# Two-block network on one core: modulation chunks loaded behind the first attention, expert weights in the state stage

## The reference, cut to what matters

```python
c_act = silu(c)
sh1, sc1, gt1, sh2, sc2, gt2 = split(c_act @ w_mod + b_mod, 6)
h = layer_norm(x) * (1 + sc1) + sh1
y = hybrid_mixer(h)       # chunked state-space scan (SSD) and forgetting attention, gated and merged, @ w_o
x = layer_norm(alpha * x + (1 + gt1) * y, ln1_g, ln1_b)
h = layer_norm(x) * (1 + sc2) + sh2
y = hierarchical_moe(h)   # 16 experts, 2 picked per token: (silu(h @ w_gate) * (h @ w_up)) @ w_down
x = layer_norm(alpha * x + (1 + gt2) * y, ln2_g, ln2_b)
```

## Time and profile before

| what | value |
|---|---|
| time, median of 3 runs | 1687.82 us |
| the three runs | 1689.45, 1684.5, 1687.82 us |
| span of the profiled execution, first to last instruction | 1684.1 us |
| its mean granted TensorE clock | 0.992 |
| PE busy | 1594.6 us |
| DVE busy | 936.2 us |
| ACT busy | 655.0 us |
| bytes read from HBM | 330.94 MB |

### The profile page before, as it was taken

One profiled execution on the slowest core, in us unless ns is written; L12 is line 12 of the kernel. 1 busy time (PEld: TensorE's weight loads), 2 busy tenths in 40 slices (PEclk: granted clock), 3 DMA queues, 4 the chain that ended last, 5 costly groups with the idle time before them and its releaser, 6 DMA issues.

```text
span 1684.1 us, 22446 instructions
## 1 busy us (share of the span) xinstructions
PE 1594.6 (95%) x9391; PEld 1239.9 (74%) x9391; DVE 936.2 (56%) x1380; ACT 655.0 (39%) x962; POOL 27.4 (2%) x89
## 2 busy tenths in 40 slices
PE   5999999989999879999999999999999999999998
PEld 1998655454445468687888899988768778889986
DVE  3876666632222266466675566545456567556653
ACT  2543420111111144565644534435355644544441
POOL 1000010100000000000000000000000000000000
PEclk9999999999999989999999999999999999999999
DMA  9555518999999924423354356545424235536651
GB/s 310 193 177 200 202 55 296 332 383 404 393 357 410 389 97 150 125 70 131 127 197 154 122 179 200 193 152 199 144 85 150 101 125 176 174 120 194 200 176 74
DMA packets 165376, 333.29 MB, mean 198 GB/s; under 512 B 17699, under 2 KB 69157, under 8 KB 165285
## 3 DMA queue, kind: packets, MB, share of 16 engines
q1 hardware_dynamic: 159728, 326.94, 54.2%
q10 hardware_dynamic: 5558, 5.06, 0.9%
HBM read 330.94 MB, written 1.05 MB: 197 GB/s over the span
## 4 chain that ended last, share of the span: by engine, by line
PE 77%; DVE 10%; DMA 7%; ACT 4%; issue 1%; POOL 0%; ACTq 0%; SPq 0%; POOLq 0%; DVEq 0%
PE ps_g L726 19%; PE ps_g L707 15%; PE ps_g L1262 5%; PE ps_g L1130 5%; DMA arena<-in_w_up_dram 4%; PE ps_s L1518 4%; PE ps_p L1518 3%; PE ps_o L774 3%; PE ps_g L867 3%; DVE ring_r L2266 2%; PE ps_p L707 2%; DMA ring<-in_w_mod_dram 1%; PE ps_x L680 1%; PE ps_g L1485 1%; PE ps_g L1406 1%
## 5 line engine op out<-in xcount | busy, mean ns | idle before, releaser
L2266 DVE TENSOR_TENSOR ring_r<-ring,late_w 128x4096 fp32r<-128x4096 f32 (+1 forms) x50 | 217.0, 4339 | 153.4 <-ACT late_w L1834 153.4
L1834 ACT ACTIVATE late_w<-ring 128x4096 fp32r<-128x4096 f32 (+1 forms) x50 | 178.1, 3563 | 126.8 <-PE ps_p L1518 42.8
L726 PE MATMUL ps_g<-hf_high,ring_r 128*128 128x256 f32 x640 | 178.9, 280 | 0.0
L726 PE MATMUL ps_g<-hf_high,late_w 128*128 128x256 f32 x576 | 162.1, 282 | 0.0
L726 PE MATMUL ps_g<-h_t_r,late_w 128*128 128x256 f32 x576 | 161.3, 280 | 0.0
L726 PEld LDWEIGHTS ps_g<-hf_high,ring_r 128*128 128x128 f32 x640 | 121.9, 190 | 0.0
L726 PEld LDWEIGHTS ps_g<-h_t_r,late_w 128*128 128x128 f32 x576 | 108.7, 189 | 0.0
L726 PEld LDWEIGHTS ps_g<-hf_high,late_w 128*128 128x128 f32 x576 | 108.1, 188 | 0.0
L1858 ACT ACTIVATE arena<-arena,neg_max 128x256 f32<-128x256 f32 (+1 forms) x160 | 71.5, 449 | 40.4 <-DVE neg_max L2321 40.4
L1130 PE MATMUL ps_g<-arena 128*64 128x512 f32 x288 | 85.9, 599 | 0.0
L707 PE MATMUL ps_g<-early_w,first_low 128*128 128x512 f32 (+1 forms) x176 | 68.7, 390 | 4.1 <-ACT arena L1820 2.2
(11 more groups left out here) (697 smaller groups left out, 3710.7 us busy)
## 6 DMA issues: line engine op xcount, KB each, us to landing
ring<-in_w_in_dram SPq DMA_DIRECT2D x31, 2048.0 KB, 7.9
ring<-in_w_gate_up_dram SPq DMA_DIRECT2D x44, 1024.0 KB, 7.4
arena<-in_w_down_dram SPq DMA_DIRECT2D x16, 2048.0 KB, 14.3
ring<-in_w_mod_dram SPq DMA_DIRECT2D x10, 2048.0 KB, 11.3
ring<-in_w_down_dram SPq DMA_DIRECT2D x10, 2048.0 KB, 7.9
arena<-in_w_up_dram SPq DMA_DIRECT2D x8, 2048.0 KB, 18.7
ring<-in_w_gate_dram SPq DMA_DIRECT2D x8, 2048.0 KB, 16.0
ring<-in_w_up_dram SPq DMA_DIRECT2D x4, 2048.0 KB, 19.1
```

What stands on the lines that cost most here:

```text
L726: ins = pe.matmul(b.ap[:, (f % 2) * SEQ:(f % 2 + 1) * SEQ], a[:, k, f * P:(f + 1) * P], x[:, k, :], start=k == 0 and i == 0, stop=k == nk ...
L1834: act.activation(high_of(name, rnd)[:, 0:n], ring[:, slot, 0:n], ACT.Copy).then_inc(high_ready.sem, 1)
L2266: dve.tensor_tensor(ring_r[:, slot, 0:n], ring[:, slot, 0:n], high_of(name, rnd)[:, 0:n].bitcast(F32), ALU.subtract).then_inc(low_ready.se ...
```

## The change

Sums: mod10 and mod11 become list chunks, loaded into the ring right behind `att`, and DVE sums them in the merges of att, one before each half. Strips: mod6 and mod7 are loaded behind them; their strips go into bank PT in the state stage, mod6's after the second turned block of x, mod7's between the segment sums of the two chunks; only the lane sums remain at the end. The list's slots are written out (`FIRST_SLOTS`), and gs1 comes behind mod7 in the list. Expert weights of pair 0 and the odd gates: down1 is loaded behind mod5, down0 behind o0 when `yo` and the decays are done, the odd gates after `yd1` and after the turned block `gy11`; gate1, up1, up0, gate0 follow o1 in that order. For this the odd gates, the second half of `odd_up`, `b_rows`, the first norm's rows and the loop's small operands get other places in the arena, and the second odd gate is one load instead of two.

```diff
-MOD_SUMMED = [8, 9, 4, 10, 11]
+MOD_SUMMED = [8, 9, 10, 11, 4]
...
-                "gs1", "mod4", "mod5", "so0", "so1", "o0", "o1", "mod6", "mod7"])
+                "mod10", "mod11", "mod6", "mod7", "gs1", "mod4", "mod5", "so0", "so1", "o0", "o1"])
+FIRST_SLOTS = [j % 3 for j in range(FIRST_CHUNKS.index("mod6"))] + [1, 2, 0, 1, 2, 0, 1, 2, 0]
+LAYER_FIRST_SLOT = 1
...
-        odd_w = arena[:, 0:SLOT].rearrange("p (k n) -> p k n", n=HALF), [arena[:, lo:lo + SLOT // 2].rearrange("p (k n) -> p k n", n=HALF) for lo in (12 * D, GATES_AT - 2 * D)]
-        odd_up = x_rows, arena[:, 14 * D:16 * D].rearrange("p (t n) -> p t n", n=D)
+        odd_w = [arena[:, lo:lo + SLOT].rearrange("p (k n) -> p k n", n=HALF) for lo in (8 * D, 12 * D)]
+        odd_up = x_rows, arena[:, GATES_AT - 2 * D:GATES_AT].rearrange("p (t n) -> p t n", n=D)
...
-        pair_y = view(at + 2 * D, 1, D)
-        expert_t = view(at + 3 * D, 2, HALF)
-        hid_t = view(at + 4 * D, KF, P)
+        pair_y = view(0, 1, D)
+        expert_t = view(D, 2, HALF)
+        hid_t = view(2 * D, KF, P)
...
-        b_rows = view(at + 1024, SSD_GROUPS, SSD_N)
+        b_rows = view(at, SSD_GROUPS, SSD_N)
...
+        def strips_bank(i):
+
+            return PT if i in (6, 7) else mod_bank(i)
...
@@ tensor: state stage, and the end of the block
                 ins.then_inc(b.full, 1)
+                if r == 1:
+                    mod_strips(6)
             claim(S, "cb")
...
             for c in range(TB):
+                if c == 1:
+                    mod_strips(7)
                 for g in range(SSD_GROUPS):
...
             product_block("o1", 1, mg_turned)
-            mod_strips(6)
-            mod_strips(7)
             strips_sum(6)
             strips_sum(7)
...
@@ sync
+            def load_odd_gate(p, e):
+
+                w = t["w_gate"][0, 2 * p + e].rearrange("(k p s) n -> p k (s n)", p=P, s=2)
+                sync.dma_start(odd_w[e].rearrange("p (k s) n -> p k (s n)", s=2), w).then_inc(odd_landed[e], 16)
...
+                if name == "mod5":
+                    sync.wait_ge(G1.full, G1.nth("first", "att1"))
+                    load_expert("down1", 0)
                 if name == "o0":
                     sync.wait_ge(S.full, S.nth("first", "yo"))
                     sync.wait_ge(decay_ready, TB * SSD_GROUPS)
-                    for j, i in enumerate(MOD_LATE):
-                        sync.dma_start(keys(pair_w[4 + j], KD, HALF), sources("first", MOD_CHUNKS[i], 0)[0]).then_inc(late_landed[j], 16)
-                if name == "mod6":
+                    load_expert("down0", 0)
+                    sync.wait_ge(PT.full, PT.nth("first", "yd1"))
+                    load_odd_gate(1, 1)
+                    sync.wait_ge(O.full, O.nth("first", "gy11"))
+                    load_odd_gate(1, 0)
+            for name in ("gate1", "up1", "up0", "gate0"):
+                if name == "up1":
                     sync.wait_ge(O.full, O.nth("first", "mg11"))
                     load_expert("up1", 0)
-                if name in ("mod6", "mod7"):
-                    j = ("mod6", "mod7").index(name)
-                    sync.wait_ge(mod_parts, MOD_SUMMED.index(MOD_LATE[j]) + 1)
-                    load_expert(f"down{j}", 0)
-            for j, name in enumerate(PAIR_CHUNKS[:SLOTS]):
-                part, use, rnd = last[j]
+                    continue
+                part, use, rnd = last[PAIR_CHUNKS.index(name)]
...
-            load_gates(1, 1, (rows.sem, rows.at("first", "h2_1")))
             load_up(1, (X.full, X.nth("first", "places")))
...
@@ scalar
+            keep_strips(6)
             for i in range(TB * SSD_GROUPS):
+                if i == SSD_GROUPS:
+                    keep_strips(7)
                 act.wait_ge(seg_cut, i + 1)
...
-            for i in (6, 7):
-                keep_strips(i)
...
@@ vector: merges of att, merges of so
             for half in range(2):
+                add_modulation(MOD_LATE[half])
                 for tb, b in enumerate(G):
                     d = gate_att[:, tb, half * HALF:(half + 1) * HALF]
...
                         ins.then_inc(rows.sem, 1)
-                    add_modulation(MOD_LATE[tb], range(i * KD // 2, (i + 1) * KD // 2))
```

More of the change, by code:

```diff
@@ L259, in place_chunks @@
 def place_chunks():
-    place, at, landed = {}, 0, [0] * SLOTS
+    place, landed = {}, [0] * SLOTS
     for part, (rounds, names) in PARTS.items():
+        slots = FIRST_SLOTS if part == "first" else [(LAYER_FIRST_SLOT + j) % SLOTS for j in range(len(names))]
         per = [0] * SLOTS
-        for j, name in enumerate(names):
-            per[(at + j) % SLOTS] += 16 * PIECES.get(name, 1) * (name != "unused")
+        for s, name in zip(slots, names):
+            per[s] += 16 * PIECES.get(name, 1) * (name != "unused")
         seen = [0] * SLOTS
-        for j, name in enumerate(names):
-            s = (at + j) % SLOTS
+        for s, name in zip(slots, names):
             seen[s] += 16 * PIECES.get(name, 1) * (name != "unused")
@@ L271, in place_chunks @@
         landed = [a + rounds * b for a, b in zip(landed, per)]
-        at += rounds * len(names)
     return place
@@ L597, in two_blocks @@
         in_dtf, half_joined = sem("in_dtf"), sem("half_joined")
-        late_landed = [sem(f"late_landed{j}") for j in range(2)]
         odd_up_landed = sem("odd_landed_up0")
@@ L820, in mod_strips @@
             def mod_strips(i):
-                name, b = MOD_CHUNKS[i], mod_bank(i)
+                name, b = MOD_CHUNKS[i], strips_bank(i)
                 biased = i < len(MOD_FIRST)
@@ L1160, in _ @@
             even_w = [[keys(pair_w[e], KD, HALF)[:, k, :] for k in range(KD)] for e in range(2)]
-            odd_gate_w = [[odd_w[0][:, k, :] for k in range(KD)], [odd_w[1][k // 4][:, k % 4, :] for k in range(KD)]]
+            odd_gate_w = [[odd_w[e][:, k, :] for k in range(KD)] for e in range(2)]
             even_up_w = [[keys(pair_w[2 + e], KD, HALF)[:, k, :] for k in range(KD)] for e in range(2)]
@@ L1168, in _ @@
                     b.again()
-                expert_pair(q + 1, [(odd_landed[e], (q * 8 + 16) * (e + 1)) for e in range(2)], odd_gate_w,
+                expert_pair(q + 1, [(odd_landed[e], q * 8 + 16) for e in range(2)], odd_gate_w,
                             [(odd_up_landed, q * 16 + 32), (expert_landed[3], q * 16 + 32)], odd_up_w)
@@ L1648, in load_gates @@
                     return
-                w = [t["w_gate"][0, 2 * p + e].rearrange("(k p s) n -> p k (s n)", p=P, s=2) for e in range(2)]
-                sync.dma_start(odd_w[0].rearrange("p (k s) n -> p k (s n)", s=2), w[0]).then_inc(odd_landed[0], 16)
-                for half, dst in enumerate(odd_w[1]):
-                    sync.dma_start(dst.rearrange("p (k s) n -> p k (s n)", s=2), w[1][:, 2 * half:2 * half + 2, :]).then_inc(odd_landed[1], 16)
+                for e in range(2):
+                    load_odd_gate(p, e)
             def load_up(p, after):
@@ L1879, in keep_strips @@
             def keep_strips(i):
-                b = mod_bank(i)
+                b = strips_bank(i)
                 act.wait_ge(b.full, b.nth("first", f"{MOD_CHUNKS[i]}s"))
@@ L1974, in _ @@
             copy_block("mg", 0, mg_turned)
-            for i, name in enumerate(["ln1_g", "ln1_b", "ln2_g", "ln2_b"]):
-                if i < 2:
-                    act.dma_start(ln_rows[:, i, :], t[name].broadcast_to([P, D])).then_inc(in_ln, 16)
+            for i, name in enumerate(["ln1_g", "ln1_b"]):
+                act.dma_start(ln1_rows[:, i, :], t[name].broadcast_to([P, D])).then_inc(in_ln, 16)
             copy_block("mg", 1, mg_turned)
-            for i in (6, 7):
-                keep_strips(i)
             for i in (6, 7):
@@ L2391, in add_modulation @@
             def add_modulation(i, ks=range(KD)):
-                if i in MOD_LATE:
-                    place, arrived, count = pair_w[4 + i - 10], late_landed[i - 10], 16
-                else:
-                    slot, count, _ = PLACE["first", MOD_CHUNKS[i]]
-                    place, arrived = ring[:, slot, :], landed[slot]
-                w, total = keys(place, KD, HALF), mod_cols(i)
-                dve.wait_ge(arrived, count)
+                slot, count, _ = PLACE["first", MOD_CHUNKS[i]]
+                w, total = keys(ring[:, slot, :], KD, HALF), mod_cols(i)
+                dve.wait_ge(landed[slot], count)
                 for k in ks:
@@ L2721, in normed @@
                 moments(tb, f"ln1_{tb}")
-                st.done(dve.scalar_tensor_tensor(x_rows[:, tb, :], resid[:, tb, :], mean_var[:, tb, 0:1], ln_rows[:, 0, :], ALU.subtract, ALU.mult))
+                st.done(dve.scalar_tensor_tensor(x_rows[:, tb, :], resid[:, tb, :], mean_var[:, tb, 0:1], ln1_rows[:, 0, :], ALU.subtract, ALU.mult))
                 st.settle()
                 dve.wait_ge(rstd_ready.sem, rstd_ready.at("first", f"ln1_{tb}"))
```

(2 more changed lines are left out.)

16 lines of the change are left out of this document (9 added, 7 removed).

## The result

The changed kernel took 1694.49 us (median of 4 runs, 1691.46 to 1697.4) beside 1686.89 us of the kernel before on the same chip. The ratio is **1.0042, 95% interval 1.0028 to 1.0055**: 7.1 us slower (0.0042 x 1686.9), between 4.7 and 9.3. The profiled execution has a span of 1689.7 us and a mean granted clock of 0.989, against 1684.1 and 0.992 before. The forecast was 1692.0 us, +4.2.

A forecast was written before the change was run, and what follows sets the result against it. The prediction took TensorE (PE), busy 95% of the span, to bound the kernel. Its terms 2.7 + 0.9 + 1.85 - 1.28 made +4.2 us, a span of 1688.3, put on the median as 1692.0 us, range 1686 to 1698.

The forecast's parts named there:

- Sums behind att: Attention merges: DVE's sums of mod10 and mod11, the first waiting for its chunk, delay the running-sums copy by 2.7 us.
- the 9.2 taken: Load queue: a mod chunk issued into an idle queue was taken to land 9.2 us after issue.
- Strips of mod6: State stage, between second and third turned x block: the strips delay the third block for DVE, costing 0.9 us.
- of mod7, +1.85: State stage, between the two chunks' segment sums: PE has no gap there, so mod7's strips cost their full 1.85 us.
- the 3 worked out: SP's queue: gs1, loaded behind mod7, lands 3 us before its use; past that each us late is lost.
- Strips gone from the end: End of the block: PE sheds strips and waiting, but DVE is next, so only 1.28 us are won.
- Expert weights: Expert stage: loading ahead was taken as worth 0, from a range of nothing to 1.5 us gained.
- 3.2 us of new idling: End of the block: PE ends the bias sums 4.5 us sooner, its next work only 1.28 sooner, so idles 3.2 us.
- a late load: Slower rival's other route: gs1 late by more than its 3 us cover; 1694 to 1698 us, chance 0.22 with the clock.
- a sign against itself: Routing stretch: the prediction said it would be wrong if the granted clock fell there.
- the forecast case: Whole kernel: the summed terms hold, giving 1692.0 us with own range 1689.5 to 1694.5; chance 0.55.
- the clock rival: Behind PE's new idling the clock falls, costing 1.7 us or nothing; 1694 to 1698 us, chance 0.22 with a late load.

The follow-up runs named there:

- e3: The changed kernel with the strips of mod6 and mod7 and their loads back at the end of the block, sums kept behind att; ratio to the kernel before 1.0019.
- e7: The changed kernel with one DVE pass in place of eight in each of the two sums behind att, loads kept; ratio to the kernel before 1.0037.
- e2: The changed kernel with the early loads of expert weights taken back, sums and strips kept; ratio to the kernel before 1.0041.
- e4: The kernel before with another order of SP's loads inside the expert loop, nothing else changed; ratio to the kernel before 0.9978.
- e10: The changed kernel with PE busy in the long wait, mod6's strips ahead of the third segment sum, and reordered expert loads; ratio to the kernel before 0.9991.
- e9: The kernel before, unchanged, profiled a second time; shift to first expert product took 23.74 us.
- e11: Second profile of the changed kernel with four matmuls computed twice more to fill PE's 4.06 us wait; shift to first expert product 20.56 us.
- e5: The kernel before with only the strips of mod6 and mod7 moved into the state stage, sums left as before; ratio to the kernel before 1.0035.
- e6: The changed kernel with four matmuls ahead of PE's 4.06 us wait computed twice more, so PE stays busy; ratio to the kernel before 1.0026.

## Why the prediction was nearly right, and what it left out

- **Sums behind att, +2.7:** +2.4 in the profiled execution, 2.4 to 3.2 over the profiles of the changed kernel and its variants (e3 with 3.9 apart). The cause is that named: DVE's passes behind a chunk that lands late (e7). That the landing is set by the queue was right too: 9.0 us after its issue, as the 9.2 taken.
- **Strips of mod6, +0.9, and of mod7, +1.85:** together 2.75, measured 2.80 (B to C), the same in five profiles. gs1 was not late: 2.6 us of cover were left of the 3 worked out.
- **Strips gone from the end, -1.28:** measured -1.24 against the first profile of before and -1.7 against the mean of four (97.57 against 99.25), because the landing of mod7 that this removes scatters: PE waited 0.67 us for it in one execution of the kernel before and 1.91 in the other.
- **Expert weights, 0:** over the pairs -0.8 in the first profile, nothing between the changed kernel and e2 (229.50 and 229.27) or between e4 and e10. The mechanism was that given: pair 2's loads hang on pair 0's gate product, and the stream idles ahead of it. A possible gain of 1.5 us ahead of the first pair, told of under e9, was not in the forecast and is not shown.
- **The step that failed** is in the rivals. The forecast saw "3.2 us of new idling" and priced a fall of the clock there at "+1.7 or nothing", as a case of its own with a chance of 0.22 (shared with a late load), outside the sum. The idling was 3.4 us (4.06 less 0.66), and the fall came, which the forecast had named as a sign against itself: in the 4 us behind this wait the clock was 0.50 to 0.58 in all six profiles that have it, and 1.00 in the seven others. Its cost is not one of two values: up to the second row block it was 2.7 us in the mean and 1.1 to 4.2 in single executions. It belonged into the sum with its mean.
- **The number:** the time, 1694.49, lies on the border between the forecast case's own range (to 1694.5) and that of the clock rival (from 1694). The stages show both at once, the forecast's terms and the rival's clock, and that the whole range held the time owes something to its width.

The stages then add up, by means over the profiles, to 2.9 + 2.8 - 1.7 + 2.7 - 1.2 = 5.5 us. Here 2.9 is the mean of A to B over the seven profiles with both full sums behind att and the strips (19.86) less 16.97, and -1.2 is the second part of D to E, in which both groups hold kernels with early and with late weights. Ahead of A and behind F no difference goes with the change: from F to the end it is 1084.7 and 1086.9 us in the two profiles of the kernel before and 1085.5 to 1088.5 in the kernels with a part of the change or all of it. The timed difference is 7.1 (4.7 to 9.3). The 1.6 us between are within the interval; whether they are scatter or, for instance, further falls of the clock in the state stage (e11 shows mod6's strips there at 3.49 us in place of 1.92) the runs don't settle. That the wait lowers the clock is shown by e5, which has it without the sums, and by e6, e10 and e11, in which it is filled and the clock stays at 1.00 over the same 4 us; the size, 2.7 us, rests on six profiles against four that don't overlap. No timed run shows it by itself: e6's ratio is lower, but on another chip and with overlapping intervals.

## What to carry to other kernels

Taking work off the bounding engine just ahead of a wait on another engine doesn't only win less than its length: it opens a longer wait, and a longer wait can halve the clock for the products behind it, so price the clock with the wait and not as an accident. Loading weights earlier gained nothing in the loop while the next loads hung on slots that freed no sooner; look at what the stream does right after, and change the order in which the in-order queue waits for slots. When single times scatter by more than the effect, cut the profiles of several executions into stages between the same two instructions: the strips' 2.80 us agreed to 0.01 us in five profiles there and could not be told in the total.

## What the hardware showed that was not expected

- A wait of 4.06 us was followed by a granted clock of 0.50 to 0.58 for between 4 and 12 us in the same program, and the 32 routing products took 3.88 us in one execution and 6.86 in another.
- The clock also fell without a long wait: the kernel before showed 0.50 and 0.69 from 344 to 352 in e9 behind waits of 0.67 and 0.34 us, in a stretch of small products, and 1.00 and 0.65 in its first profile. With PE kept busy ahead of that stretch it fell there too, for one stretch of 4 us in e6 and e11 (0.58 and 0.57, then 0.99 and 1.00) and for two in e10 (0.59 and 0.56).
- Four pairs in a row ran without a stall at 402 to 409 GB/s once the order of loads was changed (e4), so the stream as such could feed them.
- In four of thirteen profiles the products that pick the first pair's rows met a clock of 0.50 and took 3.2 to 3.7 us in place of 2.05. All four load the odd gates behind the second norm, and none of the others does; the cause is open.
